# Grouping the heads of a head norm in fours, feeding an output projection head by head, and folding the final norm into the same program

## What is computed

```python
def finish(o, z):                       # o: (B, L, 8 heads, 128)
    L = o.shape[1]
    of = o.astype(jnp.float32)
    of = of * lax.rsqrt(jnp.mean(of * of, axis=-1, keepdims=True) + SUBLN_EPS)
    of = of * subln_gain.astype(jnp.float32) * (1.0 - lambda_init)
    return (of.reshape(B, L, D).astype(z.dtype) * jax.nn.silu(z)) @ w_out
...
x_lat = x_lat + gt[:, None, :] * y_lat
...
return rms_norm_2(x_lat, final_gain)    # over the 1024 features of a token
```

## Time and profile before

| | us |
|---|---|
| median of 3 runs | 2660.18 |
| lowest and highest | 2658.41, 2670.77 |
| the profiled execution's own time | 2672.52 |
| its span, first to last instruction | 2670.5 |
| the block of `head_norm_project` begins at | 2491.3 |
| first matmul of the projection | 2543.15 |
| first instruction of the final norm's load | 2652.47 |
| mean granted clock of TensorE | 0.929 |

### The profile page before, as it was taken

The page is one execution under the profiler, slowest core; times in us unless marked ns, Lnnn a source line. Parts: engine busy times, 40 slices in busy tenths (PEclk is TensorE's granted clock), DMA queues, the critical chain, the costliest instruction groups (busy, mean ns, idle before and its releaser), DMA issues. The chain is left out here.

```text
span 2670.5 us, 31794 instructions
## 1 busy us (share of the span) xinstructions
PE 2356.1 (88%) x12468; PEld 1944.7 (73%) x12468; DVE 1133.2 (42%) x1952; ACT 957.2 (36%) x1780; POOL 865.9 (32%) x689
## 2 busy tenths in 40 slices
PE   5999476989799999999996987998999699999596
PEld 4899244977688888888885765877788588888255
DVE  4454474761322222222223244543210488888233
ACT  5434443871322112211123133221121376776330
POOL 2432152443222122312212115111111377776330
PEclk8999676999899999999997987999999899999798
DMA  4365633531111111201102103443451533533411
GB/s 127 80 166 139 219 113 100 146 76 59 51 60 50 37 48 56 63 28 48 52 16 72 32 16 91 118 107 99 122 146 67 163 88 101 148 92 79 157 48 71
DMA packets 223509, 237.25 MB, mean 89 GB/s; under 512 B 63576, under 2 KB 158312, under 8 KB 223360
## 3 DMA queue, kind: packets, MB, share of 16 engines
q1 hardware_dynamic: 155520, 195.36, 25.5%
q10 hardware_dynamic: 67840, 39.86, 5.4%
HBM read 170.06 MB, written 65.10 MB: 88 GB/s over the span
## 5 line engine op out<-in xcount | busy, mean ns | idle before, releaser
L1850 POOL TENSOR_TENSOR mlp_w_lo<-mlp_stage,mlp_w_hi 128x512 fp32r<-128x512 f32 x128 | 163.5, 1293 | 511.7 <-ACT mlp_w_hi L1862 511.3
L2478 DVE TENSOR_REDUCE da_low_score<-da_scores 128x1 f32<-128x1280 f32 x128 | 190.0, 1485 | 29.3 <-PE da_scores L2360 29.3
L326 PE MATMUL mlp_down<-mlp_w_hi,mlp_h_hi 128*128 128x512 f32 x512 | 199.2, 389 | 0.0
L326 PE MATMUL mlp_down<-mlp_w_lo,mlp_h_hi 128*128 128x512 f32 x512 | 199.2, 389 | 0.0
L326 PE MATMUL mlp_down<-mlp_w_hi,mlp_h_lo 128*128 128x512 f32 x512 | 199.2, 389 | 0.0
L1910 DVE TENSOR_TENSOR residual<-residual,mlp_down 128x512 f32<-128x512 f32 x128 | 87.9, 687 | 244.0 <-PE mlp_down L326 244.0
L2461 POOL TENSOR_TENSOR da_prob<-da_prob 128x1280 f32<-128x1280 f32 x64 | 188.3, 2942 | 5.3
L308 POOL TENSOR_TENSOR dp_w_lo<-dp_stage,dp_w_hi 128x512 fp32r<-128x512 f32 x64 | 82.2, 1288 | 332.1 <-ACT dp_w_hi L297 331.9
L2360 PE MATMUL da_scores<-da_k_hi,da_q 128*128 128x512 f32 (+1 forms) x384 | 152.0, 396 | 30.2 <-DMA da_k_lo<-dk_lo 26.2
L1862 ACT ACTIVATE mlp_w_hi<-mlp_stage 128x512 fp32r<-128x512 f32 x128 | 77.5, 621 | 269.3 <-PE mlp_down L326 226.0
L2419 ACT ACTIVATE da_prob<-da_scores,da_low_score 128x1280 f32<-128x1280 f32 x128 | 170.5, 1332 | 7.4 <-DVE da_low_score L2478 7.3
(11 more groups left out here) (383 smaller groups left out, 6557.7 us busy)
## 6 DMA issues: line engine op xcount, KB each, us to landing
mlp_stage<-in_w_mlp_up SPq DMA_DIRECT2D x64, 256.0 KB, 2.9
mlp_stage<-in_w_mlp_down SPq DMA_DIRECT2D x64, 256.0 KB, 3.0
dp_stage<-in_da_w_in SPq DMA_DIRECT2D x64, 256.0 KB, 3.2
gla_ada_w<-in_ada_w SPq DMA_DIRECT2D x12, 1024.0 KB, 5.1
da_k_hi<-dk_hi SPq DMA_DIRECT2D x32, 320.0 KB, 9.8
da_k_lo<-dk_lo SPq DMA_DIRECT2D x32, 320.0 KB, 11.3
dq<-dp_out_hi ACTq DMA_DIRECT2D x32, 256.0 KB, 3.7
da_q<-dq SPq DMA_DIRECT2D x16, 512.0 KB, 8.8
```

Source lines behind the costliest of these rows:

```text
L326: last = nc.tensor.matmul(out, x, y, start=(n == 0), stop=(n == total - 1))
L1850: nc.gpsimd.tensor_tensor(w_lo[:, which, k], stage[:, n % SLOTS], w_hi[:, which, k].bitcast(F32), ALU.subtract).then_inc(w_lo_ready, 1)
L2478: nc.vector.tensor_reduce(out=low_score[:, n, z:z + 1], in_=scores[z][:, 0:K], op=ALU.min, axis=AX.X).then_inc(low_score_ready, 1)
```

## The change

What moves:

- The heads are taken in groups of four (`PACK`), each with its own `sum_bank`, its own sums and its own Ln and Exp: four groups in all where there were two.
- The four results of a half's first feature group (g = 0) are no longer made one after the other. `by_head(half, h)` adds the three products of one head to all four banks, 12 matmuls, and waits only for the low part of that head and, in the first half, for that head's chunk of weights. Between `by_head(half, h)` and `by_head(half, h + 1)` stands the `wide` of head h + 2. The second group (g = 1) is still made result by result. There are 4 banks instead of 5.
- POOL and ACT take the 8 chunks of group 0 head by head beside the heads, and the 8 of group 1 after them. SP loads in that order, and loads `o` of the second half only behind all weight chunks.
- The final norm stands in the same block: POOL makes the inverse root of a token tile as soon as its sum is there, DVE scales it (`final`), SP stores it. The final gain is loaded into two slots of the ring of `z`, once 14 heads are multiplied by z. On DVE the first four `final` stand ahead of the `add` of the second half.

SP's list:

```diff
             for h in range(DH):
                 load_o(0, h)
...
+            for h in range(DH):
+                load_z(h)
+                w.load_chunk(sp, h)
...
+            for h in range(DH):
+                w.load_chunk(sp, DH + h)
+            for h in range(DH):
+                load_o(1, h)
+                if h % 2:
+                    load_z(DH + h // 2)
+            for n in range(DH + ZS, N):
                 load_z(n)
...
+            sp.wait_ge(y_ready, N - 2)
+            sp.dma_start(final_gain, a["final_gain_2"].rearrange("(a n) -> a n", a=1).to_broadcast([P, D]))\
+                .then_inc(final_gain_loaded, 16)
```

ACT's list (`inverse_root(p)` is Ln and Exp of a group of four):

```diff
+            for half in range(HALVES):
+                at = half * DH
+                for h in range(PACK):
+                    square(at + h)
+                inverse_root(2 * half)
+                for h in range(PACK, DH):
+                    square(at + h)
+                if half == 0:
+                    w.split_hi(act, 0)
+                high(at)
+                inverse_root(2 * half + 1)
+                for h in range(1, DH):
+                    if half == 0:
+                        w.split_hi(act, h)
+                    high(at + h)
+                if half == 0:
+                    w.split_hi_group(act, 1)
```

PE's list:

```diff
+            def by_head(half, h):
+
+                pe.wait_ge(lo_ready, half * DH + h + 1)
+                if half == 0:
+                    pe.wait_ge(w.lo_ready, h + 1)
+                for i in range(QT2):
+                    if half and h == 0:
+                        pe.wait_ge(added, QT2 + i + 1)
+                    tok = slice((half * QT2 + i) * P, (half * QT2 + i + 1) * P)
+                    for m, (x, y) in enumerate(((c.Xhi, w.hi), (c.Xhi, w.lo), (c.Xlo, w.hi))):
+                        last = nc.tensor.matmul(banks[i][:], x[:, h, tok], y[:, 0, h], start=(h == 0 and m == 0),
+                                                stop=(h == DH - 1 and m == 2), skip_group_check=True)
...
             sums(0)
...
+            wide(0)
+            wide(1)
+            sums(1)
             for h in range(DH):
-                wide(h)
-            result(0)
-            result(1)
-            sums(1)
-            result(2)
+                by_head(0, h)
+                if h + 2 < DH:
+                    wide(h + 2)
+            result(0, 0)
+            result(0, 1)
+            sums(2)
+            wide(DH)
+            result(0, 2)
+            wide(DH + 1)
+            sums(3)
+            result(0, 3)
             for h in range(DH):
-                wide(DH + h)
-                if h % 2:
-                    result(EARLY + h // 2)
...
+                by_head(1, h)
+                if h + 2 < DH:
+                    wide(DH + h + 2)
+            for i in range(QT2):
+                result(1, i)
```

DVE's list from the last head on:

```diff
+            low(N - 1)
+            dve.wait_ge(final_gain_loaded, 16)
+            for t in range(QT2):
+                final(t)
+            for n in range(2 * QT2, 3 * QT2 + 2):
                 add(n)
...
+            for i in range(2, QT2):
+                final(QT2 + i - 2)
+                add(3 * QT2 + i)
+            final(TT - 2)
+            final(TT - 1)
```

More of the change, by code:

```diff
@@ L2625, in high, with inverse_root @@
                     .then_inc(hi_ready, 1)
[L2627 to L2651, removed]
+            def inverse_root(p):
+                act.wait_ge(eps_added, p + 1)
+                if p >= 2:
+                    act.wait_ge(wide_ready, PACK * (p - 1))
+                nc.scalar.activation(rs[:, p % 2], sum_bank[p % 2][0:PACK, :], ACT.Ln, scale=1.0 / P).then_inc(logged, 1)
+                act.wait_ge(logged, p + 1)
+                nc.scalar.activation(rs[:, p % 2], rs[:, p % 2], ACT.Exp, scale=-0.5).then_inc(head_rstd, 1)
+            for half in range(HALVES):
[15 more added lines that the diff above has]
+                    w.split_hi_group(act, 1)
             for t in range(TT):
-                half, i = divmod(t, QT2)
-                act.wait_ge(added, half * PER + QT2 + i + 1)
+                act.wait_ge(added, whole(t))
                 if t:
@@ L2698, in result @@
+            def result(half, i):
+                n = half * 2 * QT2 + QT2 + i
+                pe.wait_ge(added, n - QT2 + 1)
+                tok = slice((half * QT2 + i) * P, (half * QT2 + i + 1) * P)
+                product(nc, banks[i][:],
+                        [((c.Xhi[:, k, tok], c.Xlo[:, k, tok]), (w.hi[:, 1, k], w.lo[:, 1, k])) for k in range(KT)],
                         NCOL, result_ready,
-                        (lambda k: pe.wait_ge(w.lo_ready, w.first[g] + k + 1)) if n < PER and t == 0 else None)
+                        (lambda k: pe.wait_ge(w.lo_ready, w.first[1] + k + 1)) if n == QT2 else None)
@@ L2748, in add, with final @@
                 nc.vector.tensor_tensor(c.H[:, t, cols], c.H[:, t, cols], bank, ALU.add).then_inc(added, 1)
-            for h in range(DH):
+            def final(t):
+                dve.wait_ge(rstd_ready, t + 1)
+                nc.vector.scalar_tensor_tensor(out=c.H[:, t, :], in0=c.H[:, t, :], scalar=rstd[:, t:t + 1],
+                                               in1=final_gain, op0=ALU.mult, op1=ALU.mult).then_inc(out_ready, 1)
+            scale(0)
+            for h in range(1, DH):
                 scale(h)
-                if h:
-                    low(h - 1)
+                low(h - 1)
@@ new lines, in _ @@
+            for n in range(QT2 + 2):
+                add(n)
+            scale(DH)
+            add(QT2 + 2)
+            scale(DH + 1)
+            low(DH)
+            add(QT2 + 3)
+            for h in range(2, DH):
+                scale(DH + h)
+                low(DH + h - 1)
+            low(N - 1)
[3 more added lines that the diff above has]
+            for n in range(2 * QT2, 3 * QT2 + 2):
+                add(n)
+            for i in range(2, QT2):
+                final(QT2 + i - 2)
+                add(3 * QT2 + i)
```

166 lines of the change are left out of this document (62 added, 104 removed).

## The result

The changed kernel took 2676.24 us in the median of 10 runs (2669.05 to 2680.17), the kernel before 2658.78 (2655.24 to 2670.77, 10 runs). The ratio is 1.0055, with an interval of 1.004 to 1.007: slower by 14.6 us on 2658.8. The forecast was 2669 with a range of 2648 to 2679. The time is in the range. By the 0.5% that the prediction set as its bound, it lies a hair beyond "the same", on the slower side, to which the prediction gave 0.24, and at the upper edge of A's own range of 2662 to 2676.

What follows compares the result with a forecast made beforehand. PE was taken as the bound, idle before its first projection matmul and in the tail. 29.9 us won at the start and 11.5 at the tail, against 50.1 more in the loops, gave 8.7 slower: 2669 us, range 2648 to 2679.

Steps and rivals of the forecast that it cites:

- A: The forecast: in the loops over heads the clock goes to and fro; 2669 us, 2662 to 2676, chance 0.60.
- block's start to first product: Block's start: first projection matmul at about 2513.3, 29.9 us earlier than before.
- loop of half 0: First half's loop over heads: six turns of 6.9 us and 5.4 for the last two heads, 46.8 us.
- middle: Between the loops: four results, two groups of sums, two `wide`, PE idle 2.8 for Ln and Exp; 35.9 us.
- wait at `result(1, 0)`: After the second loop: PE idle about 3.7 us for the first bank, its `add` behind four `final`.
- four results, to the last gate step: Last four results: 21.8 us, and about 1.5 for a restart at the half clock.
- tail: From the last gate step to the end of the span: 9.4 us, where before it was 20.9.
- The closed chain: Loop turn: 12 matmuls, `wide`, `scale`, `low`, PE idle through the last two; 5.33 us at full clock, 8.41 at half.
- The clock: In the loops, half the turns at each clock level: mean turn 6.9 us, granted clock about 0.75.
- B: Clock stays full through both loops, 37.4 us each: 2651 us, between 2646 and 2656, chance 0.24.
- C: Most loop turns at the half clock: slower by over 0.5%, mostly near 2680 us, chance 0.10.
- D: Late load of `o` of half 1 stalls PE 3 to 10 us at `sums(2)`: 2672 to 2679, chance 0.06.

Runs made afterwards that it cites:

- after: The changed kernel itself, as profiled: median 2676.24 us, ratio 1.0055 to the kernel before.
- full filler: Changed kernel plus six unused 128-row matmuls behind the `wide` of each of the 12 loop turns: 2658.0 us, ratio 0.9987 to the kernel before.
- thin filler: Changed kernel plus one unused four-row fp32 matmul behind the `wide` of each of the 12 loop turns: 2678.8 us, ratio 1.0061 to the kernel before.
- the fold alone: Kernel before with only the final norm taken into the same block, its tiles between the last adds: 2645.0 us, ratio 0.9945.
- the chain opened alone: Changed kernel with `wide` of head h + 2 moved ahead of head h's 12 matmuls in both loops: 2639.8 us, ratio 0.9924 to the kernel before.
- the other two moves: On the changed kernel with `wide(h + 2)` early: four adds ahead of the first `final` tiles, `wide(8)` behind `result(0, 2)`; all three 2628.6 us, ratio 0.9880.
- low first: Changed kernel with `low(h - 1)` ahead of `scale(h)` on DVE in both loops: 2647.8 us, ratio 0.9941 to the kernel before.
- Adds first: Changed kernel with four adds of the second half's first group ahead of the first four `final` tiles: 2667.3 us, ratio 1.0033 to the kernel before.

## Why the prediction was right, and where its sizes were off

The path of the prediction, stage by stage, beside what the trace of after shows:

| stage | predicted | measured | difference |
|---|---|---|---|
| block's start to first product | 22.0 | 22.7 | +0.7 |
| loop of half 0 | 46.8 | 46.4 | -0.4 |
| middle | 35.9 | 41.1 | +5.2 |
| loop of half 1 | 46.8 | 47.8 | +1.0 |
| wait at `result(1, 0)` | 3.7 | 5.1 | +1.4 |
| four results, to the last gate step | 23.3 | 24.1 | +0.8 |
| tail | 9.4 | 7.9 | -1.5 |
| block | 187.9 | 195.2 | +7.3 |

The last product of a loop is counted to its end here, so the wait is PE's idle time of 5.1 and not the 5.3 of the other table.

**The closed chain** was right, and both ways of opening it show it: `wide`, `scale`, `low` and the gap before the next products, 12 times with the gap of 1.44 (predicted 1.6). Its price at full clock was put at 5.33 a turn, and the full filler measures 5.51; with the clock of after it is 7.1, put at 6.9.

**The clock** came out at 0.82 and 0.79, where the prediction expected about 0.75, and in the order that it named: 0.50 behind a stretch with little but `wide` and a gap (2514.04 to 2517.46), and 1.00 again with the products still running. One detail was wrong. I took half of the turns at each level and turns of 5.3 or 8.5; every turn but the first has both levels in it. The half itself was an assumption between two limits, and no row gave it; that the mean turn came out at 7.1 by the trace and at 6.9 by the sum is in part luck. The choice between rivals A and B rested on the earlier trace rows, where eight-row matmuls did not raise the clock (0.50), and the thin filler confirms that reading (0.81), with the full filler as its counterpart (1.00). No row showed that gaps as short as the loop's would lower the clock; the traces have 0.50 and 1.00 within a turn of 7.1 us with gaps of 1.44 and, in the thin filler, within one of 7.01 with gaps of 0.59. The GHz that the prediction and the expectations write for the two levels stand in no run: the traces give the clock as a share alone, 1.00 and 0.50, and the products 0.23 and 0.42 apart.

**The step that was mis-sized is the middle**, 5.2 of the 7.3. The prediction had PE idle 2.8 ahead of `wide(8)` and it was 2.62; but it put the matmuls behind that wait at the full clock. In after `wide(8)` and the first ten of them ran at 0.50 (2568.7 to 2575.5): 3.3 more. It had charged such a restart at `result(1, 0)`, and not here. The two waits for chunks of group 1 came to 1.34 (0.29 and 1.05), which the prediction had named ("by a us at most") without a term in the sum. Some 0.7 is left in small terms.

**The wait for the bank** was 5.1 instead of 3.7, ended by DVE's add behind the four `final`, as said. The sum gave 11.2 from `scale(15)` to the end of that add; it is 2642.70 - 2629.10 = 13.6. DVE's timeline has `scale(15)`, the first and the fourth tile, and the end of the add. The tiles are 1.75 to 2.0 apart where I had 1.25, each waiting for POOL:

```profile
2629.10 0.75 DVE L2771 SCALAR_TENSOR_TENSOR hp_o<-hp_o,hp_gain,hp_wide 128x512 f32<-128x512 f32 x1 [5.62 <-PE hp_wide L2707]
...
2634.32 1.28 DVE L2793 SCALAR_TENSOR_TENSOR residual<-residual,hp_rstd,hp_z 128x1024 f32<-128x1024 f32 x1 [1.35 <-POOL hp_rstd L2620]
...
2640.08 1.28 DVE L2793 SCALAR_TENSOR_TENSOR residual<-residual,hp_rstd,hp_z 128x1024 f32<-128x1024 f32 x1 [0.72 <-POOL hp_rstd L2620]
...
2642.01 0.69 DVE L2789 TENSOR_TENSOR residual<-residual,hp_ps 128x512 f32<-128x512 f32 x1
```

I had taken POOL's inverse roots as 0.2 + 0.7 per tile, which fits beside a `final`; the last section has what they took.

**The tail** is 1.5 shorter than put, since the end of the span follows the last `final` sooner; the gain is 13.0 instead of 11.5, and the fold alone gives the same 13.0.

**From block to median.** The profiled execution of before was longer than its median by 12 (by 14 when ten runs are taken); that of after was at its median. The block's growth (16.0), the ratio (14.6) and the difference of medians (17.5) agree within what single executions scatter; the prediction carried 8.8, short by the terms above.

**The rivals.** B (full clock throughout, 2651) fell with the windows of 1.00 and 0.50 in one turn. The full filler gives its price from the other side: 2658.0, with the middle 0.9 longer than in after and the wait for the bank 1.6 longer. C (mostly half clock) fell too: no turn was at 0.50 throughout, and the mean clock of the loops, 0.82 and 0.79, was above the forecast's. The time went past the 0.5% bound by A's own small terms. D (a late load of half 1) didn't occur: PE's waits have no entry for it, and `sums(2)` followed `result(0, 1)` without a stall.

**Where the expected gain went.** The early start of the products did come: 22.7 us into the block instead of 2543.15 - 2491.3 = 51.9, 29 us, and so did 13.0 at the tail. The loops gave back 94.1 - 43.5 = 50.6, and the waits ahead of `wide(8)` and of the bank cost 6.9 + 6.8 = 13.7 with their stretches at 0.50, less the six `wide` that moved from the later stages into the loops (6 x 1.07 = 6.4). Together: -29.2 - 13.0 + 50.6 + 13.7 - 6.4 = +15.7, against 16.0 between the blocks. With the chain opened alone the loops take 56.7 and the same idea is worth 0.8%; with the other two moves it is 1.2%.

## What to carry to other kernels

When work of two engines is interleaved by hand, follow one item around both lists: if engine X does A(n+2) behind B(n), engine Y does C(n+1) behind the step that needs A(n+2), and B(n+1) needs C(n+1), the loop runs at the sum of all its steps, though no engine looks full (here 5.51 a turn at the full clock, and about 4.0 with the chain cut). Cut it at whichever joint is easier; issue the small step for a later item ahead of the big one for this item.

A pause of TensorE can cost more than its length where products follow it: here 5.1 us cost 6.8, 2.6 us cost 6.9, and 12 gaps of 1.44 cost 12 x 1.44 = 17.3 and another 16.7 through the clock. It is not certain either: in "low first" the wait of 2.6 us left the clock at 1.00. So look at the granted clock beside every stall, and put adds that free banks ahead of work for which nobody waits.

Try the plain part of a combined change alone: the fold was worth 13 us, and the reordering beside it hid that. The fold and the opened order together were worth 32 us of the block (179.2 to 147.1).

## What the runs showed that I had not expected

POOL's one-column instructions took up to nearly seven times as long beside DVE's `final`. POOL's timeline, mean and power of the first tiles:

```profile
2633.37 0.19 POOL L2617 TENSOR_SCALAR hp_mean<-sums 128x1 f32<-128x1 f32 x1 [1.79 <-ACT hp_sq L2678]
...
2634.62 1.03 POOL L2617 TENSOR_SCALAR hp_mean<-sums 128x1 f32<-128x1 f32 x1 [0.41 <-ACT hp_sq L2678]
...
2636.65 1.39 POOL L2620 TENSOR_TENSOR hp_rstd<-hp_mean,minus_half 128x1 f32<-128x1 f32 x1
2638.13 1.28 POOL L2617 TENSOR_SCALAR hp_mean<-sums 128x1 f32<-128x1 f32 x1
```

The mean takes 0.19 with DVE idle, 1.03 and 1.28 when it begins inside a `final` (2634.32 to 2635.60, 2638.08 to 2639.36), and both end within 0.05 us of that `final`'s end. One mean that began 0.05 after a `final` did (2636.38) still took 0.19, but then the power behind it took 1.39, where the others take 0.55 to 0.57. The five other traces with the first `final` ahead of the adds show the same, 1.03 to 1.29 for a mean begun inside a `final`. "Adds first" shows the other side. There DVE is busy with `add` when POOL works on the third and fourth tile, and the `final` come later:

```profile
2637.25 0.19 POOL L2617 TENSOR_SCALAR hp_mean<-sums 128x1 f32<-128x1 f32 x1 [0.40 <-ACT hp_sq L2678]
```

It begins inside the gate step of 2637.06 and takes 0.19; all eight means of that run do, and the powers 0.55 to 0.57. So beside `add` POOL keeps its pace and beside `final` it doesn't. Which property of `final` does it (its form, its 1024 columns, its operands) no run separates.

PE "busy" and PE at the full clock were two things here: with a second four-row matmul in the gap, PE was busy for 36.49 of 40 us and had a mean of 0.81, while the end of the attention, busy for 10.93 of 17, and "low first", busy for 24.02 of 25, had 1.00. And 72 useless matmuls of 128 rows made the kernel faster by 13.5 us in the block.

The clock came out of phase with the work: 1.00 during `wide` and all but at most 0.4 us of the gap, and 0.50 for 3.0 to 3.4 us of the products behind them, in every turn but the first. In the loops that cost 16.7 of 94 us, nearly all of it out of the 72 products per loop that follow such a gap.
